# Seams of a two-block kernel: the v halves around q and k, late store waits, half tiles, and a last chunk on VectorE

## The reference, cut to what matters

```python
proj = xn @ w_in                       # qk, v, o, i_pre, f_pre, u, sv, gates
qk = silu(conv4(qk)); q, k = split(qk)
h = mlstm_chunkwise(q, k, v, i_pre + b_i, f_pre + b_f)   # 8 chunks of 128 tokens, 4 heads of 256
y_a = rmsnorm(h) * sigmoid(o)
y_b = spatial_gating(u, sv)
out = (sigmoid(gate_a) * y_a + sigmoid(gate_b) * y_b) @ w_out
```

## Time and profile before

| | us |
|---|---|
| median of 3 runs | 2838.73 (2833.31, 2838.73, 2839.36) |
| the profiled execution | 2833.47 |
| its span | 2831.6 |
| PE busy | 2567.1 (91% of the span) |
| DVE, ACT, POOL busy | 1308.2, 1184.4, 642.6 |
| mean granted clock of PE | 0.96 |

### The profile page before, as it was taken

One profiled execution on the slowest core, in us unless ns is written; L12 is line 12 of the kernel. 1 busy time (PEld: TensorE's weight loads), 2 busy tenths in 40 slices (PEclk: granted clock), 3 DMA queues, 4 the chain that ended last, 5 costly groups with the idle time before them and its releaser, 6 DMA issues. The chain is left out here.

```text
span 2831.6 us, 30827 instructions
## 1 busy us (share of the span) xinstructions
PE 2567.1 (91%) x12104; PEld 2084.0 (74%) x12104; DVE 1308.2 (46%) x1705; ACT 1184.4 (42%) x1709; POOL 642.6 (23%) x525
## 2 busy tenths in 40 slices
PE   7999988879899999989997869898994999999992
PEld 6888866668687878868886758785683888888881
DVE  5530227754213212130445633104216888888885
ACT  4212137763241212122322532324322777777773
POOL 2313203323121213132211553245111111111100
PEclk9999999999999999999998989999996999999996
DMA  5433045522210131132215522233245899999985
GB/s 174 149 123 111 31 119 134 135 77 95 97 60 30 45 119 60 60 83 97 80 62 169 167 96 95 105 122 133 79 170 193 328 374 379 381 383 382 374 358 211
DMA packets 168562, 455.78 MB, mean 161 GB/s; under 512 B 17792, under 2 KB 85536, under 8 KB 155744
## 3 DMA queue, kind: packets, MB, share of 16 engines
q1 hardware_dynamic: 118768, 385.51, 37.9%
q10 hardware_dynamic: 36720, 40.64, 4.1%
q0 software_dynamic: 12928, 27.63, 2.8%
HBM read 389.23 MB, written 82.31 MB: 167 GB/s over the span
## 5 line engine op out<-in xcount | busy, mean ns | idle before, releaser
L2594 DVE TENSOR_TENSOR ex_w_lo<-ex_w,ex_w_hi 128x2048 fp32r<-128x2048 f32 x198 | 448.1, 2291 | 82.3 <-ACT ex_w_hi L2539 79.3
L2539 ACT ACTIVATE ex_w_hi<-ex_w 128x2048 fp32r<-128x2048 f32 x198 | 379.0, 1915 | 52.1 <-PEq L2140 26.4
L219 POOL TENSOR_TENSOR p_w_lo<-w_raw,p_w_hi 128x512 fp32r<-128x512 f32 (+1 forms) x154 | 202.9, 1347 | 649.1 <-ACT p_w_hi L239 623.6
L219 POOL TENSOR_TENSOR p_w_lo_rest<-w_raw,p_w_hi_rest 128x512 fp32r<-128x512 f32 x94 | 122.9, 1339 | 266.8 <-ACT p_w_hi_rest L239 266.8
L264 PE MATMUL o_ps<-o_w_hi,o_m_hi 128*128 128x512 f32 x384 | 154.7, 403 | 19.9 <-POOL split_cols L1027 19.9
L266 PE MATMUL o_ps<-o_w_hi,split_cols 128*128 128x512 f32 x384 | 153.0, 398 | 0.0
L265 PE MATMUL o_ps<-o_w_lo,o_m_hi 128*128 128x512 f32 x384 | 152.7, 398 | 0.0
L264 PE MATMUL p_ps<-p_w_hi,hT_hi 128*128 128x512 f32 (+1 forms) x320 | 120.9, 378 | 0.0
L239 ACT ACTIVATE p_w_hi<-w_raw 128x512 fp32r<-128x512 f32 (+1 forms) x133 | 74.5, 599 | 106.6 <-DMA w_raw<-w_in 30.9
L266 PE MATMUL p_ps<-p_w_hi,hT_lo 128*128 128x512 f32 (+1 forms) x320 | 118.5, 370 | 0.0
L265 PE MATMUL p_ps<-p_w_lo,hT_hi 128*128 128x512 f32 (+1 forms) x320 | 118.3, 370 | 0.0
(11 more groups left out here) (431 smaller groups left out, 6506.5 us busy)
## 6 DMA issues: line engine op xcount, KB each, us to landing
ex_w<-w SPq DMA_DIRECT2D x99, 2048.0 KB, 14.0
w_raw<-w_in SPq DMA_DIRECT2D x42, 1024.0 KB, 5.2
x_rows<-o_x SPq DMA_DIRECT2D x24, 512.0 KB, 2.6
att_k<-k_columns SPq DMA_DIRECT2D x46, 256.0 KB, 7.6
w_raw<-w_out SPq DMA_DIRECT2D x8, 1024.0 KB, 10.0
qk_columns<-qk_y ACTq DMA_DIRECT2D x16, 512.0 KB, 2.6
ml_qk<-qk_columns SPq DMA_DIRECT2D x8, 1024.0 KB, 6.4
o_x<-x_rows SPq DMA_DIRECT2D x16, 512.0 KB, 3.8
```

Of the source, the lines that this page charges most:

```text
L219: emit(self.lo(n)[:, 0:w], self.half(n // (KC // 2), w)[:, n % (KC // 2), :], self.hi(n)[:, 0:w].bitcast(F32), ALU.subtract).then_inc(self ...
L2539: nc.scalar.activation(w_hi[:, n % RING, :], raw_half(n), ACT.Copy).then_inc(hi_done, 1)
L2594: nc.vector.tensor_tensor(w_lo[:, n % RING, :], raw_half(n), w_hi[:, n % RING, :].bitcast(F32), ALU.subtract).then_inc(down_lo if m == "w2 ...
```

## The change

Five edits in the second block, one of them in all three output products:

1. `project_out`: tile 0 is rounded by ACT in two halves and its rest is taken by DVE, in two halves, in place of POOL. ACT doesn't wait for `eps` before it. PE's first four slices wait for the first half only.
2. `spatial_gate` and `output_gate` no longer wait for their stores; ACT in the next stage waits (before its first eviction), and in `project_qkv` DVE too, before its first memset.
3. `project_qkv`: the order of the panels is v's first half, q and k, v's second half. The exponentials come behind group `g0 + 12`, and the row steps before the group's eviction.
4. `mlstm`: PE waits for `start` after the first scores, the carry and the turned keys. Each chunk of q and k is loaded as two DMAs, q and k; for chunk 0 the one of k is issued by ACT.
5. `mlstm`: the last chunk is scaled and multiplied by `og` (four operations of 128x256) and added to `yb` by DVE; POOL and ACT no longer do this for that chunk.

```diff
@@ project_out
             @block.gpsimd
                 for t in range(NT):
-                    pool.wait_ge(rounded, t + 1)
-                    nc.gpsimd.tensor_tensor(tile(cols, t), tile(plain, t), m_hi[:, t % 2, :, :].bitcast(F32),
-                                            ALU.subtract).then_inc(rest, 1)
+                    if t >= 1:
+                        pool.wait_ge(rounded, t)
+                        nc.gpsimd.tensor_tensor(tile(cols, t), tile(plain, t), m_hi[:, t % 2, :, :].bitcast(F32),
+                                                ALU.subtract).then_inc(rest, 1)
...
+                            if t == 0 and n == 0 and k % (KC // 2) == 0:
+                                pe.wait_ge(first_lo, 1 + k // (KC // 2))
...
+                for half in range(2):
+                    nc.scalar.activation(first_part(m_hi[:, 0, :, :], half), first_part(plain, half), ACT.Copy
+                                         ).then_inc(first_hi, 1)
+                round_hi(1)
                 act.wait_ge(eps_ready, 1)
-                round_hi(0)
-                round_hi(1)
...
+                for half in range(2):
+                    dve.wait_ge(first_hi, half + 1)
+                    nc.vector.tensor_tensor(first_part(cols, half), first_part(plain, half),
+                                            first_part(m_hi[:, 0, :, :], half).bitcast(F32), ALU.subtract
+                                            ).then_inc(first_lo, 1)
@@ mixer_weights
-    a, b = row_panels(w, V_AT, len(sources))
-    sources, groups = sources + a, groups + b
+    values(0)
     for n in range(2 * D // BANK):
...
+    values(1)
@@ spatial_gate, output_gate
-                sp.wait_ge(y_out, 16 * NT)
...
-                sp.wait_ge(out, 16 * NT)
...
                 weights.before(act, span.start)
+                act.wait_ge(y_out, 16 * NT)
@@ project_qkv
-                    if g == n_v:
+                    if g == n_q + 8:
                         pe.wait_ge(row_weights, 1)
...
-                    if g == g0 + 10:
+                    if g == n_q + 4:
                         act.wait_ge(diffs, 1)
...
                 weights.before(act, g0)
+                act.wait_ge(og_out, 16 * NT)
...
+                    row_step(g)
+                    if g < n_q or g >= n_v:
...
+                        if g == n_v + 1:
+                            silu(NSUB - 1)
...
-                silu(NSUB - 1)
...
             def _(dve):
+                dve.wait_ge(og_out, 16 * NT)
@@ mlstm
-                        sp.dma_start(qk[:, t % 3, :, :], qk_dram[:, :, t * P:(t + 1) * P].rearrange("j p n -> p j n")
-                                     ).then_inc(qk_in[t % 3], 16)
+                        load_chunk(sp, t, 0, KC)
+                        if t > 0:
+                            load_chunk(sp, t, KC, 2 * KC)
...
-                pe.wait_ge(start, 1)
                 scores(0)
                 spread_carry(0)
                 turn_keys(0)
+                pe.wait_ge(start, 1)
...
+                def mix_last():
+                    t = NT - 1
+                    dve.wait_ge(og_in[t % 2], 16 * (t // 2 + 1))
+                    dve.wait_ge(yb_in, 16 * NT)
+                    dve.wait_ge(rstd_ready, NT)
+                    for h in range(MH):
+                        m, at = hh[:, t % 2, h * MD:(h + 1) * MD], slice(h * MD, (h + 1) * MD)
+                        ins = nc.vector.scalar_tensor_tensor(m, m, ss[:, 2, h:h + 1], og[:, t % 2, at], ALU.mult, ALU.mult)
+                    c.vstep(dve, ins)
+                    nc.vector.tensor_tensor(hh[:, t % 2, :], hh[:, t % 2, :], yb[:, :], ALU.add).then_inc(m_ready, 1)
...
                 invert_rms(NT - 1)
+                mix_last()
...
+                load_chunk(act, 0, KC, 2 * KC)
                 act.wait_ge(start, 1)
...
-                scale_rows(NT - 1)
                 keep_mixed(NT - 1)
```

More of the change, by code:

```diff
@@ L980, in tile, with first_part @@
             return buffer[:, :, t * P:(t + 1) * P]
+        def first_part(buffer, half):
+            return buffer[:, KC // 2 * half:KC // 2 * (half + 1), 0:P]
         with nc.Block() as block:
@@ L1053, in _ @@
                 for t in range(NT):
-                    pe.wait_ge(rest, t + 1)
+                    if t >= 1:
+                        pe.wait_ge(rest, t)
                     if t >= 2:
@@ L1161, in mixer_weights, with values @@
             sources.append(([by_rows(w, at + n * BANK, at + (n + 1) * BANK)], BANK))
-    a, b = row_panels(w, V_AT, len(sources))
-    sources, groups = sources + a, groups + b
+    def values(n):
+        groups.extend((len(sources), "rows", 0, BANK, t) for t in range(NT))
+        sources.append(([by_rows(w, V_AT + n * BANK, V_AT + (n + 1) * BANK)], BANK))
+    values(0)
     for n in range(2 * D // BANK):
@@ L1168, in mixer_weights, with spatial_gate @@
         sources.append(([by_rows(w, n * BANK, (n + 1) * BANK)], BANK))
+    values(1)
     return Weights(c, stack, "p2", sources, groups, pre=6, first=6)
 SGU_PANELS, GATE_PANELS, QKV_PANELS = (0, 6), (6, 10), (10, 16)
-def spatial_gate(c, weights, hT, yb_dram):
+def spatial_gate(c, weights, hT, yb_dram, y_out):
     nc, io = c.nc, c.io
@@ L1296, in _, with output_gate @@
                         nc.vector.tensor_tensor(y, y, gb[:, (g - 1) % NB, :], ALU.mult).then_inc(gated, 1)
-def output_gate(c, weights, hT, og_dram):
+def output_gate(c, weights, hT, og_dram, y_out, out):
     nc, io = c.nc, c.io
@@ L1312, in output_gate @@
         done, freed = weights.done, weights.freed
-        bias_in, gate_ready, gated, out = c.sem("og_bias_in"), c.sem("og_gate_ready"), c.sem("og_gated"), c.sem("og_out")
+        bias_in, gate_ready, gated = c.sem("og_bias_in"), c.sem("og_gate_ready"), c.sem("og_gated")
         with nc.Block() as block:
@@ L1378, with project_qkv @@
 C_A, C_FLOOR, C_WS = range(3)
-def project_qkv(c, weights, hT, qk_dram, v_dram, maxima, carry, cols, decay):
+def project_qkv(c, weights, hT, qk_dram, v_dram, maxima, carry, cols, decay, og_out):
     nc, io = c.nc, c.io
@@ L1506, in _ @@
                         act.dma_start(v_rows[t, :, n * BANK:(n + 1) * BANK], v_sb[:, slot, :]).then_inc(v_out[slot], 16)
-                        row_step(g)
-                    else:
-                        j, half = divmod(g - n_v, 2)
-                        if g == n_v:
+                        if g == n_v + 1:
+                            silu(NSUB - 1)
+                    else:
+                        j, half = divmod(g - n_q, 2)
+                        if g == n_q:
                             act.wait_ge(small_in, 16 * (TAPS + 1))
@@ L1618, in mlstm, with load_chunk @@
         rms_ready, m_ready, m_kept = c.sem("ml_rms"), c.sem("ml_m_ready"), c.sem("ml_m_kept")
+        def load_chunk(engine, t, j0, j1):
+            engine.dma_start(qk[:, t % 3, j0:j1, :], qk_dram[j0:j1, :, t * P:(t + 1) * P].rearrange("j p n -> p j n")
+                             ).then_inc(qk_in[t % 3], 16)
         with nc.Block() as block:
@@ L2762, in build @@
                     hT = Halves(cols, hT_lo)
-                    spatial_gate(c, mixer, hT, yb)
-                    output_gate(c, mixer, hT, og)
+                    yb_out, og_out = c.sem("sgu_y_out"), c.sem("og_out")
+                    spatial_gate(c, mixer, hT, yb, yb_out)
+                    output_gate(c, mixer, hT, og, yb_out, og_out)
                     rows = front.enter_context(ExitStack())
@@ L2769, in build @@
                     decay = rows.enter_context(nc.sbuf_tensor("ml_decays", [P, MH, NT], F32, side="right"))
-                    project_qkv(c, mixer, hT, qk2, v2, maxima, carry, ml_cols, decay)
+                    project_qkv(c, mixer, hT, qk2, v2, maxima, carry, ml_cols, decay, og_out)
                 with ExitStack() as left:
```

31 lines of the change are left out of this document (16 added, 15 removed).

## The result

| | before | after |
|---|---|---|
| median | 2838.29 (2833.31 to 2839.36, 4 runs) | 2812.65 (2811.98, 2812.59, 2812.72, 2818.92) |
| the profiled execution | 2833.47 | 2812.59 |
| its span | 2831.6 | 2810.8 |
| PE busy | 2567.1 | 2565.9 |

The ratio is 0.992, with a 95% interval from 0.9908 to 0.9932: the change makes the kernel 0.8% faster (0.9% by the medians alone). PE's busy time is 1.2 us shorter, the span 20.8: nearly all of the gain is PE standing still for less.

A forecast was written before the change was run, and what follows sets the result against it. PE's idle holes at stage seams bound the kernel. Terms 6.6 + 5.3 + 6.5 + 0.5 + 2.0 = 20.9 us gave 2812.6 from the profiled execution, 2817.8 from the median; forecast 2815 us, the middle, range 2805 to 2826.

The forecast's parts named there:

- rival 2: Before output_gate: the clock stays up over the 3.1 us hole; sum 23.3 us, time 2812.6 us; chance 0.15.
- First tile in halves: Start of the three output products: PE starts 1.4 us after ACT instead of 3.62; 2.2 us per stage, 6.6 in all.
- Stores: Ends of spatial_gate and output_gate: both SP store waits go, 3.0 and 2.3 us; 5.3 us gained, holes 3.1 and 5.6.
- v around q and k: End of the q/k/v stage: the last store is issued 5.9 us sooner and lands 0.6 faster; 6.5 us gained.
- Rival 4: In the q/k/v stage: DVE's row chain and the convolutions collide, making it slower, above 2838.7 us; chance 0.03.
- Start of `mlstm`: PE's moved wait alone gains nothing; loading the first chunk by two queues lands it earlier; 0.5 us, bounds +2.5 and -1.5.
- Last chunk on DVE: End of mlstm: DVE mixes the last chunk in place of ACT and POOL; 2.0 us taken, between 0.4 and 5.1.
- "free": End of mlstm: DVE's last-chunk products run unhindered at 0.35 us each; the stage ends 5.1 us earlier.
- "full alternation": End of mlstm: DVE's five operations alternate with POOL's weight operations; the stage ends only 0.4 us earlier.
- rival 1: End of mlstm: DVE and POOL alternate fully, 0.4 us gained there; sum 19.3 us, time 2816.6 us; chance 0.2.
- Rivals 3 and 5: Former: half given back at another seam, 2821.7 us, chance 0.12; latter: new ACT waits replace the removed ones, 2822.7 us, 0.05.
- One of the signs of being wrong: Between the seams: the stages get longer, listed among the observations that would show the prediction wrong; no size given.

The follow-up runs named there:

- the last two runs: Against the changed kernel: gate weights' products one group later, 2811.79 us; that plus POOL's slices two chunks earlier and ten idle products at spatial_gate's end, median 2807.52 us.

## Why the prediction was right

The forecast was 2815, halfway between 2812.6 (the sum from the profiled execution) and 2817.8 (from the median); the median is 2812.65 and the profiled execution 2812.59. Between the profiled executions the gain is 20.9 us, and the traces explain it: 21.4 at the seams for 20.9 forecast, so the terms were right, two of them for reasons that were not quite theirs. Between the medians it is 25.6; the other 4.7 us stay open, and that the median fell on the profiled execution's sum is luck. The forecast took the kernel before to lie at two levels; its seven executions beside the last two runs spread from 2834.75 to 2842.32, six of them evenly within 3 us, and don't bear that out. The measured time is also the one of rival 2, whose mechanism did not happen: only the seams tell the two apart.

- **First tile in halves: right.** 2.26 us a stage, 2.2 forecast; taking it back gave 6.8 us. ACT, DVE, PE in 1.50 us; the second half was never waited for.
- **Stores: right.** 5.3 us, shown by the run with both waits. The holes are 3.1 and 5.6 as written. The clock stayed up through the 3.1 us hole and fell with PE's restart (0.55 in the first 3.8 us of the stage). So rival 2 did not happen; `output_gate` became 0.7 us shorter, where rival 2 had 2.4.
- **v around q and k: right.** 6.4 us, and no cost inside the stage. The row chain ended at 1262.4 and the first convolution started at 1280.3: 18 us of room where 15 were forecast. Rival 4 had nothing to work on.
- **Start of `mlstm`: right in kind, the term too small.** 1.1 for 0.5. The moved wait is worth nothing, as written. What I called a small lever is a large one: with the split chunk on one queue the first score comes 4.0 us later. The sentence "bandwidth, not the issue, is the limit" was not the whole of it, and the shares that the prediction gave to the queues (half, then two thirds) are not what happened: POOL's packets had not begun when most of the chunk moved, and once they had, SP's queue was left with 48 of 388 GB/s. The gain is the 90 KB that stood behind POOL's packets in the kernel before and no longer do.
- **Last chunk on DVE: the size right, the reason wrong.** 2.0 forecast, 1.8 measured. The forecast took a value between "free" and "full alternation", with the gain in the chunk being ready sooner. The alternation was full, as in rival 1, and DVE waited 1.2 us for `yb` besides, which the step did not have (it let DVE start behind its reciprocal, as it did in the kernel with tile 0 taken back, where the distance is 1.05 us shorter); the chunk was turned 0.27 us later. The gain came from another place: when POOL is last, 2.65 us pass until the next stage's first issue, and 1.28 when ACT is. Rival 1, which had a chance of 0.2, was the right mechanism. Its 0.4 us is what the engines' ends moved by (0.43), and it left out the hand-over to the next stage.
- **Rivals 3 and 5** did not happen: 1.4 us was given back inside the q/k/v stage and 2.1 behind o3's start, far from half; and the new waits on ACT and DVE held up nothing, as the run with the old waits shows (no other seam moved by more than 0.1 us). Rival 5's 13 us also left out the two terms of `mlstm`, which it had no reason to drop.
- **One of the signs of being wrong came** without the prediction being wrong: the q/k/v stage got longer, by a second stretch at the lower clock. No edit taken back brings the 285.9 us of the kernel before back; it is 285.7 in the kernel with ten idle products at the end of `spatial_gate`, where that stretch is missing.

## What to carry to other kernels

Where one engine paces a row of stages, write down the distance from its last instruction of one stage to its first of the next, and cut what is in it: here 21.4 of the 22.9 us up to the third output product lay in such distances. Put the piece of work whose result travels shortest last in a stage, and let nothing that can be done earlier (weight slices) stand at its end, above all not on POOL and beside a DVE operation on two SBUF tiles. Look at the size of the packets when two queues load at once: beside packets of 4096 B an urgent load in packets of 512 B got an eighth of the bandwidth here, so have it through before they begin. And judge an edit of a few us by such distances, not by the whole time of one run, which moves by more than that with the clock.

## What the runs showed of the hardware

- The loss to the low clock behind one and the same seam differs from kernel to kernel. Summed as length times missing share of the clock, `mlstm`'s first stretch lost 6.8 us in the kernel after, 8.5 with `start` first and 10.2 with the last chunk mixed by POOL, with the same work in it. An edit elsewhere can seem to cost or gain 3.4 us this way.
- In a hole of 3.1 us the granted clock stayed at 1.00 and fell to 0.50 as PE restarted; ten products of 128x512 (2.4 us) in the hole kept it up in the stage behind too. In the kernel with four filled holes it still fell within waits of 4.6 and 5.8 us.
- The end of a stage costs 2.65 us when POOL's operation ends last and 1.28 when ACT's does (2.64 with the mix taken back, 1.28 with POOL's slices early), read from the recorded ends of their last operations.
- A POOL cast and subtraction that DVE's product meets also get longer (0.60 to 0.80 and 1.26 to 1.32 us), so both sides pay.
- Two queues whose packets were of 512 B shared the DMA engines evenly (164 and 166 GB/s); a queue with packets of 4096 B left one with packets of 512 B 48 GB/s beside its own 340. The first score came 9.78 us behind SP's first issue where 361 KB of the chunk were left when the large packets began, 6.93 with 90 KB left and 5.80 with 1.
- DMAs that POOL issued 0.46 us behind SP's first moved their first packet at 3.61, 4.58 and 5.05 us in three kernels; what sets this is open.
